# A matmul with 100 weight columns in front of nine runs of 256-column matmuls per layer, in a two-layer decoder kernel on one core

## What is computed

```python
def _swiglu(x, w_gate, w_up, w_down):
    return (jax.nn.silu(x @ w_gate) * (x @ w_up)) @ w_down

def _hybrid_mixer(x, pos, ...):
    z = x @ w_in
    (c_q, c_kv, k_r, mq, mk, mv, mi, mf, mo, rq, rk, rv, rg, gl) = _split_cols(z, IN_SPLITS)
    y_mla = _mla_attention(...)                                     # 4 heads, from c_q, c_kv, k_r
    y_mlstm = jax.nn.sigmoid(mo) * _head_norm(h_ml, ...)            # 4 heads, from mq, mk, mv, mi, mf
    y_ret = jax.nn.silu(rg) * _head_norm(h_rt, ...)                 # 4 heads, from rq, rk, rv
    gate = jax.nn.sigmoid(gl.reshape(b, s, N_BRANCH, D_MODEL) + gate_b)
    merged = (gate[:, :, 0] * (y_mla @ w_br_mla)
              + gate[:, :, 1] * (y_mlstm @ w_br_mlstm)
              + gate[:, :, 2] * (y_ret @ w_br_ret))
    return merged @ w_out
```

## Time and profile before

| | us |
|---|---|
| median of 3 runs | 1280.67 (1280.36 to 1281.38) |
| the profiled execution, its own time | 1281.61 |
| its span, first to last instruction | 1279.3 |
| PE busy | 1267.8 (99% of the span) |
| DVE busy | 914.0 (71%) |
| ACT busy | 639.8 (50%) |

### The profile page before, as it was taken

The page is one execution under the profiler, slowest core; times in us unless marked ns, Lnnn a source line. Parts: engine busy times, 40 slices in busy tenths (PEclk is TensorE's granted clock), DMA queues, the critical chain, the costliest instruction groups (busy, mean ns, idle before and its releaser), DMA issues.

```text
span 1279.3 us, 18375 instructions
## 1 busy us (share of the span) xinstructions
PE 1267.8 (99%) x7864; PEld 1136.5 (89%) x7864; DVE 914.0 (71%) x1108; ACT 639.8 (50%) x658; POOL 69.8 (5%) x59
## 2 busy tenths in 40 slices
PE   9999999999999999999999999999999999999997
PEld 6888889998999988888888888899989998888886
DVE  6666569999685686666686666699977756866665
ACT  5444445694645455444454444465846354544441
POOL 0299000000000000000000000000000000000000
PEclk9999999999999999999999999999999999999999
DMA  8865647643666566556556655466436665676551
GB/s 300 265 185 189 196 135 225 200 150 100 197 213 196 188 194 219 183 192 196 167 195 231 194 184 186 161 198 199 149 100 201 228 198 165 197 230 192 186 186 62
DMA packets 178144, 240.82 MB, mean 188 GB/s; under 512 B 8264, under 2 KB 147152, under 8 KB 177936
## 3 DMA queue, kind: packets, MB, share of 16 engines
q1 hardware_dynamic: 177680, 238.08, 57.9%
q0 software_dynamic: 240, 1.44, 0.3%
q10 hardware_dynamic: 144, 0.13, 0.1%
HBM read 238.59 MB, written 1.06 MB: 187 GB/s over the span
## 4 chain that ended last, share of the span: by engine, by line
PE 92%; DVE 4%; ACT 2%; DMA 1%; issue 0%; DVEq 0%; SPq 0%
PE ps L1513 22%; PE ps L1538 22%; PE ps L1521 11%; PE ps L1446 10%; PE ps L1444 10%; PE ps L1445 10%; PE ps L1504 5%; DVE wlo L860 1%; PE ps L1466 1%; ACT whi L568 1%; PE ps L1725 1%; DMA raw<-ffn_w_up 1%; ACT sc L668 0%; DVE ml_qk L1069 0%; ACT rot_sw L654 0%
## 5 line engine op out<-in xcount | busy, mean ns | idle before, releaser
L860 DVE TENSOR_TENSOR wlo<-raw,whi 128x2048 fp32r<-128x2048 f32 (+1 forms) x218 | 492.4, 2276 | 186.5 <-ACT whi L568 186.0
L568 ACT ACTIVATE whi<-raw 128x2048 fp32r<-128x2048 f32 (+1 forms) x218 | 412.9, 1898 | 268.8 <-DMA raw<-w_in 103.6
L1513 PE MATMUL ps<-xpair,whi 128*128 128x512 f32 x1216 | 290.0, 391 | 0.0
L1513 PEld LDWEIGHTS ps<-xpair,whi 128*128 128x128 f32 x1216 | 225.8, 188 | 45.1
L1444 PE MATMUL ps<-xpair,whi 128*128 128x256 f32 x800 | 224.5, 281 | 0.0
L1446 PE MATMUL ps<-xpair,wlo 128*128 128x256 f32 x800 | 223.1, 279 | 0.0
L1445 PE MATMUL ps<-xpair,whi 128*128 128x256 f32 x800 | 223.0, 279 | 0.0
L1521 PEld LDWEIGHTS ps<-xpair,wlo 128*128 128x128 f32 x1216 | 154.5, 189 | 6.1
L1521 PE MATMUL ps<-xpair,wlo 128*128 128x256 f32 x1216 | 156.5, 282 | 0.0
L1445 PEld LDWEIGHTS ps<-xpair,whi 128*128 128x128 f32 x800 | 150.7, 188 | 0.3
L1444 PEld LDWEIGHTS ps<-xpair,whi 128*128 128x128 f32 x800 | 150.2, 188 | 0.3
(11 more groups left out here) (232 smaller groups left out, 1619.4 us busy)
## 6 DMA issues: line engine op xcount, KB each, us to landing
raw<-w_in SPq DMA_DIRECT2D x60, 1024.0 KB, 5.2
raw<-ffn_w_down SPq DMA_DIRECT2D x44, 1024.0 KB, 4.8
raw<-ffn_w_gate SPq DMA_DIRECT2D x40, 1024.0 KB, 5.4
raw<-ffn_w_up SPq DMA_DIRECT2D x40, 1024.0 KB, 5.4
raw<-w_br SPq DMA_DIRECT2D x12, 1024.0 KB, 5.0
raw<-w_out SPq DMA_DIRECT2D x8, 1024.0 KB, 4.8
g_row<-ln_rows SPq DMA_DIRECT2D x6, 512.0 KB, 6.4
b_row<-ln_rows SPq DMA_DIRECT2D x6, 512.0 KB, 7.1
```

The source lines that it names most:

```text
L568: act.activation(unit(whi, n), unit(raw, n), ACT.Copy).then_inc(w_hi, 1)
L860: dve.tensor_tensor(w_low(n), unit(raw, n), unit(whi, n).bitcast(F32), ALU.subtract).then_inc(w_lo, 1)
L1513: pe.matmul(ps[:, bank, :], wh[:, kk, cols], xpair[:, kk, :, :], start=kk == 0, stop=kk == KC - 1, skip_group_check=True)
```

## The change

A helper `narrow` issues one fp32r matmul with 100 weight columns (the first 100 columns of the unit's second block of high weights) and 256 moving columns, into partitions 0 to 99 of the first half of the bank that the following run overwrites from its first matmul on. It stands behind the waits of the unit that it precedes, and brings no wait of its own. It is called nine times per layer: ahead of the last up unit in each of the two FFNs, ahead of `c0`, `rq0`, `rq1` and `rk1`, ahead of the first gate unit of branch 0, and ahead of both branch units of branch 0. The fp32 matmul at line 1913 goes. PE has 5088 instructions in place of 5072.

```diff
+NARROW = 100
...
+        def narrow(bank, n, width, x):
+
+            pe.matmul(ps[0:NARROW, bank, 0:SEQ], slot(n, width)[0][:, 1, 0:NARROW], x, start=True, stop=True)
...
                         pe.wait_ge(w_lo, done_no(up))
+                        narrow(FFN_UP, up, 256, x_h(1))
                         two_chunks(FFN_UP, up).then_inc(w_used, 1)
...
-            def project(m, job):
+            def project(m, job, narrow_first=False):
 
                 pe.wait_ge(w_lo, done_no(m0 + m))
+                if narrow_first:
+                    narrow(BANK[job], m0 + m, 256, x_h(1))
                 two_chunks(BANK[job], m0 + m).then_inc(w_used, 1)
...
-            project(2, "c0")
+            project(2, "c0", narrow_first=True)
...
-            project(12, "rq0")
+            project(12, "rq0", narrow_first=True)
...
-            project(13, "rq1")
+            project(13, "rq1", narrow_first=True)
...
-            project(15, "rk1")
+            project(15, "rk1", narrow_first=True)
...
+                        if b == h == i == 0:
+                            narrow(GATE_BANK[i], k, 256, x_h(1))
                         two_chunks(GATE_BANK[i], k).then_inc(w_used, 1)
...
                     elif h:
                         pe.wait_ge(branch_added, turn * 4 + 3)
-                        pe.matmul(ps[:, BRANCH_BANK[0], 0:SEQ], ones, resid[:, 0, 0:SEQ], start=True, stop=True)
...
+                    if b == 0:
+                        narrow(BRANCH_BANK[0], k, 512, yhi[:, b, 1, :])
```

## The result

| | before | after |
|---|---|---|
| median, us | 1280.70 (1280.22 to 1281.39) | 1285.47 (1284.41 to 1286.65) |
| the profiled execution, its own time | 1281.61 | 1285.49 |
| its span | 1279.3 | 1283.2 |

The changed kernel takes 1.0036 of the time before (95% interval 1.0026 to 1.0046). It is slower by 4.8 us, where 2.7 us less was forecast. On the scale of the profiled executions the difference is 3.9 us.

What follows compares the result with a forecast made beforehand. PE, busy 99% of the span, was taken as the bound. 2 x (0.39 + 0.10 + 0.49 + 0.31) + 0.15 = 2.73 us off 1281.61 gave 1278.9 profiled, median 1277.9; range 1277.1 to 1285.1.

Steps and rivals of the forecast that it cites:

- The second branch unit: Exchanging line 1913 for a narrow matmul saves 0.31 us per layer, the 624 matmuls behind staying at 113.
- rival (a): A narrow matmul doesn't turn runs behind fp32 transposes; the 624 fall to 118, time 1284.7; chance 0.18.
- c0 and the gate units: Narrow matmuls turn both runs to 113: 0.39 us per layer at c0, 0.28 on PE at the gate run.
- The zero for c2's 100-column block and for qk0: After c0 and c1: neither a gain at c2's 100-column block (+0.12) nor a loss at qk0 (-0.21) was counted.
- Rival (c): Narrow works at some places, second branch unit included, but not behind 512-column matmuls; 1279.4, no change; chance 0.14.
- The gate's gain: Of 0.28 us saved on PE, 0.10 per layer stays; the rest becomes the transposes' wait for DVE's `hn`.
- The first branch unit: The run of 144 matmuls behind the head transposes turns to 113, gaining 0.49 us per layer.
- The last up units: In the FFNs, 48 matmuls ahead of 512-column ones turn to 113; 0.04 us each, four times, 0.15 in all.
- rq0, rq1, rk1: Attention part: no gain or cost, as ACT and DVE set the chain; stretch to line 1699 unchanged at 37.2 us.
- The rule of the Trainium skill: Matmul distance depends on moving columns alone, 109 ns for 256, so the change could only cost; weighed as opposing the forecast.

Runs made afterwards that it cites:

- swap_only: Kernel before, only with line 1913's fp32 matmul exchanged for one 100-column matmul ahead of the second branch unit; 1286.3 us, 1.0039 of before.
- eight_more: Same kernel as `eight`, measured over 11 executions; 1280.03 us, 0.9995 of before.
- four: Kernel before plus `narrow` ahead of c0 and the first gate unit, and four in place of line 1913; 1280.25 us.
- eight: Kernel before plus `narrow` ahead of c0 and the first gate unit, and eight in a row in place of line 1913; 1279.59 us, one execution.
- pitch_eight: `eight` with c2's 228-column block loaded as 256 columns per row; 1280.13 us, 0.9993 of before.
- again: The changed kernel, unaltered, run once more for a second profile; 1285.29 us.
- keep_1913: Changed kernel with line 1913's fp32 matmul kept and no narrow one at the second branch unit; 1280.69 us, 1.0 of before.
- width_128: Kernel before plus one matmul ahead of c0 and the first gate unit, with 128 weight columns instead of 100; 1286.52 us, one execution.
- c2_pitch: Kernel before plus `narrow` ahead of c0 and the first gate unit, c2 laid out with 256 columns per row instead of 228; 1279.10 us.

## Why the prediction was wrong

**The second branch unit** is the step that failed. It took the exchange as worth 0.31 us "if the narrow one does what line 1913 does for the 624 matmuls behind it". It doesn't: 0 of 6 such runs were at 113, in the changed kernel's two profiles and in `swap_only`'s. The stretch was 2.44 longer per layer, which is to the digit what rival (a), given a chance of 0.18, had for it (2.75 less 0.31), and w_out took 0.22 more on top. The 0.31 itself was right: the unit's second matmul (362.61) comes 1.11 us behind the start of the transposes in place of 1.42 (362.56 to 363.98 in the earlier trace rows). What it was tied to was not. The argument against the rival was that only the nearest neighbour counts, "and the narrow one is then the neighbour in both cases". `eight_more` against `four` and `swap_only` shows this to be false: the neighbour is the same 100-column matmul in all three, with 113 in 6 of 6 runs behind eight (with `eight` and `pitch_eight`) and in 0 of 6 behind one, so what stands ahead of it counts too. The two cures that the trace had were behind 24 in a row, as the prediction itself said. There was also a lopsided stake in it: 0.31 to win per layer against 2.44 to lose, at the one place where a known cure was taken out.

**c0 and the gate units**: right in mechanism. All 22 runs of c0 and all 22 of the gate units, in the eleven profiles that have the 100-column matmul there, have their 128-column matmuls of c0, c1 and of the gate units at 113; none of the ten and ten does in the profiles without it or with another form. c0 gave 0.33 in place of 0.39, the difference being mostly c2's first block, which the sum had at 113 with the rest (24 x 0.0044 = 0.11), while the narrow matmul's distance of 0.113 and the missing entry cost gave some of it back. The zero for c2's 100-column block and for qk0 held. Rival (c) is excluded.

**The gate's gain** was clipped as told, and more. The transposes took 1.30 us (layer 0) and 1.35 in place of 1.03. The chain of waits of the changed kernel shows what released them:

```profile
343.81 0.70 DVE hn L1211
344.51 0.04 issue
344.55 0.66 PE ps L1752 x4
```

DVE's `hn` ends at 344.51, and the fifth transpose starts with 0.04 of issue behind it. Of 0.31 saved at the gate units 0.04 and 0.00 were left, where I took 0.10: 0.27 and 0.31 turned into this wait. In `again`, the same program, it was 0.14 and 0.05, so this too is one draw.

**The first branch unit** was the second wrong term: 0.49 per layer expected, 0.51 gained in layer 0 and 0.13 lost in layer 1. Over the profiles with one narrow matmul ahead of the 144 (changed kernel twice, `keep_1913`) one run of six is at 113. Over those with nothing but the transposes ahead of it, it is 9 of 22. With the second branch unit's 0 of 6 that is 1 of 12 behind the head transposes and one narrow matmul. It brought nothing there, and may even have hindered, which these counts are too few to show. The 0.51 was luck. That "behind 128-column fp32 matmuls not a single run is at 113" was true of the one profile that there was; of all sixteen it is true of four (the kernel before, `swap_only`, `width_128`, `c2_pitch`).

**The last up units**: the 48 took 5.66 us as before, with 0.12 for the narrow one ahead:

```profile
175.75 0.28 PE L1486 MATMUL ps<-xpair,whi 128*100 128x256 f32 x1
175.87 0.28 PE L1445 MATMUL ps<-xpair,whi 128*128 128x256 f32 x1
...
181.53 0.39 PE L1543 MATMUL ps<-whi,hhi 128*128 128x512 f32 x1
```

None of twelve such runs in the three profiles turned. Behind these 16 matmuls of 256 columns at 118 one narrow matmul did nothing: 0.5 us lost where 0.15 gained was expected. It is the place most like c2 and qk0 in the trace of before, and there the narrow ones ahead were 24.

**rq0, rq1, rk1**: right. The stretch was to stay at 37.2 us from the copy of `q_nope` to the value products of line 1699 (now 1707), and it did, though in layer 0 rq0 and rq1 went from 118 to 113 and rk0, which the change doesn't touch, from 113 to 118. The chain of waits and then PE's timeline, after:

```profile
250.64 0.13 PE ps L1447
250.79 0.60 ACT q_nope L655
```

```profile
288.00 0.70 PE L1707 MATMUL ps<-pt,v_mla 128*128 128x256 f32 x2
```

288.00 - 250.79 = 37.21, before 37.20. rq0 in layer 1, at 113 in the earlier trace rows, was at 118 in both profiles of the changed kernel with a narrow matmul ahead of it. Beside the chain that was free.

The profiles show more here than the prediction asked. rq1 stands behind fp32 transposes as the branch units do, and with one narrow matmul ahead it was at 113 in 5 of 6 cases (changed kernel twice, `keep_1913`), without it in 2 of 26. rk0, ahead of which nothing was ever put in, was at the other pace than the rq1 before it in all 32 cases; rk1 was at the other pace than rk0 in all 26 cases without a narrow matmul ahead and at the same in all 6 with one. So a run entered from fp32 matmuls is not everywhere a fresh draw: here its pace went with that of the run before it, and at rk1 one narrow matmul changed which of the two it went with.

**By its own sum**: per layer -0.33 - 0.02 - 0.19 + 2.43 + 0.22 = +2.1 on average, twice 4.2, where -1.29 stood. Of the 3.4 per layer between the two 2.75 is the second branch unit, 0.30 the first, 0.22 w_out.

**The rule of the Trainium skill** that was weighed there, "TensorE: Matmul & The Clock Gate", section "Back-to-back issue gap" (N/2.4 + 2.5 ns, 109 ns for 256 columns), would have had the change only cost. The same section of the Trainium skill gives this for the isolated matmul and says that in a stream of weight loads and matmuls both set the distance, which the prediction left out. By the sign the rule came out right, but not by its reason: what was lost is a change of pace, which that rule doesn't have, and c0 gained by a 100-column matmul what the rule excludes.

## What to carry to other kernels

When a change takes out an instruction behind which a long run goes well, and puts in another that was seen to help elsewhere, price the place as if the new one did nothing, and try that exchange apart from the rest. What a trace shows of a state that an execution can fall into at a place is one draw; count over several executions, or over the spread of their times, before a rule is made of it. And read paces from the starts or the mean record length of long runs, since 0.0044 us a matmul was 2.75 us here while PE's busy share stayed at 99%.

## What the hardware showed that was not expected

- fp32r matmuls of 128 weight and 256 moving columns have two paces in this kernel, 0.1134 and 0.1178 us (records of 276 and 281 ns), at a granted clock that is the same for both (0.998 to 1.000). A run keeps its pace over 624 matmuls and 13 units. The first 48 of w_out's 512-column matmuls have two as well, 0.2289 and 0.2334, which don't simply follow the pace ahead of them.
- One matmul with 100 weight columns behind a run of 512-column matmuls turned the next run to 113 in 44 of 44 cases; with 128 or 64 weight columns, or with 64 moving ones, in none.
- Behind fp32 matmuls the pace can differ between executions of one program (`again` against the first profile, `eight` against `eight_more`). With nothing else ahead 9 of 22 runs of the 144 were at 113; with line 1913 ahead of the 624 13 of 16; with four 100-column matmuls 2 of 2 in the profile but, by the times, probably not in each execution; with eight all that were seen, 6 of 6 in profiles and, by the times, in 22 executions of two kernels.
- In the attention part the paces were tied to each other: rk0 was at the other pace than rq1 in 32 of 32 cases.
- A block whose weight rows lie 912 bytes apart was at 118 in a run at 113, in 16 of 16 cases; with the rows 1024 bytes apart it was at 113, in 6 of 6.

What in TensorE has these two states, why 100 columns and 912 bytes bear on it, and why the same pair of matmuls works at the first branch unit and not at the second, no run here shows. Nor does any show whether the second branch unit's one narrow matmul fails to help or itself brings 118: for that the place would have to run with neither it nor line 1913. All of this stays open.
